# The samples' block compressor as rounded high and low parts, with the pages held stationary

## The chip, the cores and the metric

The kernel runs on one core of a Trainium2 chip. The metric is the device time of one execution in microseconds (us). TensorE (PE in the profile, its weight loads PEld) multiplies, VectorE (DVE), ScalarE (ACT) and GpSimd (POOL) work elementwise, and SyncE (SP) issues all DMAs of this stage.

## What is computed

The reference is one inference step of a two-layer decoder trunk: 1024 prompt tokens, and 8 samples of 8 new tokens each with 1024 cached tokens in 8 pages. In each layer, attention heads work beside an RWKV-7 recurrence. One attention branch reads compressed blocks. The part that the change touches is this:

```python
def compress_blocks(rows, pe, w1, w2):
    b, length = rows.shape[:2]
    n_cmp = (length - CMP_BLOCK) // CMP_STRIDE + 1        # blocks of 32 rows, stride 16: 63
    idx = jnp.arange(n_cmp)[:, None] * CMP_STRIDE + jnp.arange(CMP_BLOCK)[None, :]
    blocks = jnp.take(rows, idx, axis=1) + pe[:, None, :]
    flat = blocks.transpose(0, 1, 3, 2, 4).reshape(b, n_cmp, NSA_KV_HEADS, CMP_BLOCK * HEAD_DIM)
    return jax.nn.silu(flat @ w1) @ w2
...
    k_cmp = compress_blocks(kv_all[:, :, 0], pe[0], w1[0], w2[0])
    v_cmp = compress_blocks(kv_all[:, :, 1], pe[1], w1[1], w2[1])
```

For keys and for values, and for each of two head groups, 63 blocks of 32 x 64 = 2048 numbers go through w1 (2048 x 256), SiLU and w2 (256 x 64). All is float32.

## The kernel before

Each layer runs four stages, one after the other with a barrier between: `projections`, `scan_with_samples`, `prompt_mixing` (the prompt's attention) and `dense_layer`. The change lies in the second, which holds three programs: the scan of the recurrence over the prompt (8 pairs of chunks, 19 steps a pair), the samples' attention (`sample_...`), and a short one for the samples' own chunk of the recurrence (`chunk_...`). Each program is a generator on each engine, and `turns` (L911) fixes their order in advance: 10 rounds of chunk and scan steps, and after them one scan step and one sample step in each round. An engine carries out its list strictly in order, so an instruction that waits holds all that stand behind it.

In a pair's 19 scan steps, steps 1 and 2 are gram steps (L1282 to L1294), step 3 multiplies by G (L1304), steps 4 to 13 are matrix steps of 32 products (L1314 and L1326 in turn, with ScalarE's copy L1387 after the one and VectorE's sum and transpose L1459, L1461 after the other), and steps 14 to 19 are three for each chunk (L1334; L1341; L1348 to L1358).

The samples' program goes over nine requests: eight samples and, as the ninth, the prompt, of which only the compressor runs. A request is 16 steps. Its compressor runs in the first eight:

- SyncE loads a request's pages ahead, into `sa_kvp` (two buffers).
- GpSimd (`sort_rows`, L1817) sorts their keys and values into `sa_kvc`, all four (key or value, group) parts in four copies of 512 elements, while the request before is still in its later steps.
- TensorE turns them (L1529): 8 transposes in each of steps 0 and 1. ScalarE (L1646) and VectorE (L1734) copy each half from PSUM to `sa_kt`.
- TensorE multiplies (L1540): for keys and values, for each half of the 256 hidden columns, 16 fp32 products with a 128 x 128 piece of `cp_w` (w1) stationary and 126 columns of `sa_kt` moving, laid over steps 2 to 7. The hidden values come out with the hidden index on the partitions, which is what w2 needs.
- ScalarE applies SiLU (L1658) into `sa_hid`, with the bias that comes from pe and w1 (`weigh`, L1708), and TensorE multiplies by w2 (L1567, L1571) in step 8.

Meanwhile the prompt's queries and keys (`qT`, `ksT`, `kwT`) and its values (`vs`, `vw`) lie in SBUF untouched, since `prompt_mixing` reads them. At the end of the ninth request SyncE loads the constants and rows which that stage needs first (L1499, L1500). The other matrix stages already work in high and low parts: a float32 number is rounded to fp32r (the high part) and what is left is the low part, and three products replace one: high x high, low x high, high x low. In `projections`, L538 is such a product, with a slice of the input stationary and 256 or 280 columns of weights moving.

Of the kernel before, what the change touches and what calls it, by code (L numbers as in the profile page):

```python
# [21 lines left out]
F32R = mybir.dt.float32r  # L22
# [5 lines left out]
P = 128  # L28
# [879 lines left out]
ROWS_IN = 16 * (PAGES + 3)  # L908

# [14 lines left out]
def scan_with_samples(nc, ps, cst, l, first, first_in, early, early_in, rows_early_in, scan_kept, wend, kcz, vcz, qT, gate, ptab, A, O, X):  # L924
# [8 lines left out]
    sample_names = ("row_in0 row_in1 sorted q_sorted cm_in gates_in prepared weighed bias_done bias_kept k_turned k_even k_odd hidden hid_ready sel_turned "  # L933
# [7 lines left out]
    with Scope(nc) as sc, stage(nc, f"{scan_names} {sample_names} {chunk_names}") as (block, *sems):  # L941
# [7 lines left out]
        (row_in0, row_in1, sorted_, q_sorted, cm_in, gates_in, prepared, weighed, bias_done, bias_kept, k_turned, k_even, k_odd, hidden, hid_ready, sel_turned,  # L949
# [8 lines left out]
        region = sc.sb("sc_region", [P, 13600])  # L958
        kvp2, kvc, kt, ksT, wT = sc.place(base, (("sa_kvp", [P, 2, 4, 1024]), ("sa_kvc", [P, 4, 4, P]), ("sa_kt", [P, 4, 8, 64]), ("sa_ksT", [P, 2, 512]), ("sa_wT", [P, 272])))
# [10 lines left out]
        egmask, seqt, seqp = (eoff[name] for name, _ in parts)  # L970
        w1 = sc.sb("cp_w1", [P, 2, 16, 256])
        w2 = sc.sb("cp_w2", [P, 2, 2, HD])
# [511 lines left out]
        def sample_sync(sp):  # L1484
# [3 lines left out]
            for c in range(NB + 1):  # L1488
# [5 lines left out]
                for n in range(7 if c == NB else 9):  # L1494
                    yield
                if c == NB:
                    sp.wait_ge(hidden, 4 * (NB + 1))
                    a = CO[MIX_CONSTANTS[0]][0]
                    sp.dma_start(early[0][:, :], const_d[:, a:a + MIX_WIDTH]).then_inc(early_in, 16)  # L1499
                    load_ahead(sp, early, rows_early_in, l, A, X)  # L1500
                    yield
                    yield
                    return
# [5 lines left out]

        def sample_tensor(pe):  # L1510
# [3 lines left out]
            for c in range(NB + 1):  # L1514
                u = c % 2
                kvp, wk, kn, wn = kvp2[:, u], wk2[:, u], kn2[:, u], wn2[:, u]
                for i in range(2):
                    if i == 0:
                        pe.wait_ge(sorted_, c + 1)
# [4 lines left out]
                    else:  # L1524
                        pe.wait_ge(w1_in, 96)
                    for kg in (2 * i, 2 * i + 1):
                        for n in range(4):
                            o = (4 + kg) * BANK + n * P
                            m = pe.transpose(ps[:, o:o + P], kvc[:, n, kg, :], cst["ident"])  # L1529
# [1517 lines left out]
```

## Time and profile before

| | |
|---|---|
| median of 3 runs | 3989.98 us (3989.86 to 3991.4) |
| profiled execution | 3985.85 us, its span 3984.1 us |
| granted clock, mean of the span | 0.981 of 2.4 GHz |
| busy: TensorE, VectorE, ScalarE, GpSimd | 3807, 2006, 1124, 1701 us |
| scan stage of the first layer | up to about 846 us |
| first page transposes, first and second layer | 431.96 and 2409.28 us |

A row of the profile's groups names the line of the kernel, the engine, the operation, what is written and what is read, and the count; then busy time and the mean of one; then the time the engine idled just before, and what ended it. A matmul's recorded duration includes the way through the array, so pitches are read from starts. An fp32 product is recorded as two.

### The profile page before, as it was taken

The numbers are of one execution on the slowest core, as the hardware profiler recorded it, in microseconds if no ns is written. First come the engines' busy times: TensorE is split into PE (matmuls) and PEld (weight loads), VectorE is DVE, ScalarE is ACT, GpSimd is POOL, SyncE is SP. The second block draws the span as 40 slices with busy tenths as digits, with TensorE's granted clock in tenths as the row PEclk, the third lists the DMA queues.
The fourth block names the chain that finished last, engine by engine and source line by source line (L and its number), as shares of the span: only waits on it lengthen the run. The fifth ranks groups of instructions, "written<-read, shape, count | busy, mean of one in ns | idle before, by whom it ended". The sixth has DMA issues, their size and how long they took to land. (4 is left out here: it accounts for less than half of the span.)

```text
span 3984.1 us, 83564 instructions
## 1 busy us (share of the span) xinstructions
PE 3807.4 (96%) x34199; PEld 3487.8 (88%) x34199; DVE 2006.2 (50%) x4501; ACT 1124.3 (28%) x2486; POOL 1701.1 (43%) x2284
## 2 busy tenths in 40 slices
PE   8998999989999999999999989999899999999998
PEld 8987788866699999999999877888665999999998
DVE  6587544457545414414556874444574454144153
ACT  3154233347731000100212532333477210000012
POOL 5633222136754434434355421222377644344342
PEclk9998999999999999999999999999999999999998
DMA  4255433220042131131323554332200411311313
GB/s 131 85 163 168 130 88 87 70 97 7 13 124 66 43 127 54 43 138 40 113 93 92 162 172 107 85 88 71 96 9 12 139 54 45 136 43 57 124 39 99
DMA packets 204334, 349.62 MB, mean 88 GB/s; under 512 B 73410, under 2 KB 138050, under 8 KB 203074
## 3 DMA queue, kind: packets, MB, share of 16 engines
q1 hardware_dynamic: 203954, 344.29, 27.7%
q8 instruction: 271, 4.44, 0.5%
q14 instruction: 109, 0.89, 0.1%
HBM read 253.03 MB, written 95.90 MB: 88 GB/s over the span
## 5 line engine op out<-in xcount | busy, mean ns | idle before, releaser
L2644 POOL CAST wr_hi<-wr_raw 128x256 fp32r<-128x256 f32 x584 | 262.8, 450 | 894.3 <-PE ps L2680 888.8
L2646 POOL TENSOR_TENSOR wr_lo<-wr_raw,wr_hi 128x256 fp32r<-128x256 f32 x584 | 548.6, 939 | 46.7
L2680 PE MATMUL ps<-xh,wr_hi 128*128 128x384 f32 x2064 | 453.7, 328 | 0.0
L2680 PE MATMUL ps<-xh,wr_lo 128*128 128x384 f32 x2064 | 453.1, 327 | 0.0
L2680 PE MATMUL ps<-xl,wr_hi 128*128 128x384 f32 x2064 | 452.9, 327 | 0.0
L1409 POOL TENSOR_TENSOR rc_CT<-rc_AT,rc_masks 128x256 f32<-128x256 f32 x192 | 135.6, 724 | 527.6 <-DVE rc_AT L1444 409.3
L2747 ACT ACTIVATE de_c<-de_c 128x1088 f32<-128x1088 f32 (+1 forms) x44 | 49.1, 1116 | 1098.1 <-DVE de_c L2857 1098.1
L2680 PEld LDWEIGHTS ps<-xh,wr_hi 128*128 128x128 f32 x2064 | 348.9, 188 | 0.3
L2680 PEld LDWEIGHTS ps<-xl,wr_hi 128*128 128x128 f32 x2064 | 349.0, 188 | 0.0
L2680 PEld LDWEIGHTS ps<-xh,wr_lo 128*128 128x128 f32 x2064 | 348.7, 188 | 0.0
L2680 PE MATMUL ps<-de_mixh,wr_hi 128*128 128x384 f32 (+1 forms) x1440 | 317.8, 329 | 8.1 <-DVE de_mixl L2782 8.1
L2680 PE MATMUL ps<-de_mixh,wr_lo 128*128 128x384 f32 (+1 forms) x1440 | 317.4, 329 | 0.0
L2680 PE MATMUL ps<-de_mixl,wr_hi 128*128 128x384 f32 (+1 forms) x1392 | 308.5, 329 | 0.0
L2797 DVE TENSOR_TENSOR de_x<-de_x,ps 128x384 f32<-128x384 f32 x168 | 79.3, 527 | 448.0 <-PE ps L2680 448.0
L1540 PE MATMUL ps<-sa_kt,cp_w 128*128 128x126 f32 x2304 | 285.7, 280 | 0.0
L1540 PEld LDWEIGHTS ps<-sa_kt,cp_w 128*128 128x128 f32 x2304 | 265.3, 192 | 7.3
L2243 POOL TENSOR_SCALAR at_s<-at_s,at_fac,gate 128x384 f32<-128x384 f32 (+3 forms) x320 | 209.8, 668 | 126.2 <-DVE at_fac L2225 124.9
L2680 PEld LDWEIGHTS ps<-de_mixh,wr_hi 128*128 128x128 f32 x1440 | 246.8, 189 | 8.6 <-issue 8.6
L2680 PEld LDWEIGHTS ps<-de_mixh,wr_lo 128*128 128x128 f32 x1440 | 247.6, 188 | 0.0
L2680 PEld LDWEIGHTS ps<-de_mixl,wr_hi 128*128 128x128 f32 x1392 | 235.7, 188 | 0.0
L538 PE MATMUL ps<-pr_wh,xh 128*128 128x256 f32 (+1 forms) x720 | 214.7, 298 | 4.2 <-ACT pr_turns L714 2.7
L538 PE MATMUL ps<-pr_wl,xh 128*128 128x256 f32 (+1 forms) x720 | 207.0, 287 | 0.0
(453 smaller groups left out, 7555.2 us busy)
## 6 DMA issues: line engine op xcount, KB each, us to landing
sa_kvp<-in_cache SPq DMA_DIRECT2D x128, 256.0 KB
scr_xres<-de_x SPq DMA_DIRECT2D x56, 544.0 KB, 2.7
de_x<-scr_xres SPq DMA_DIRECT2D x56, 544.0 KB, 3.6
wr_raw<-in_w_gate SPq DMA_DIRECT2D x42, 512.0 KB, 3.6
wr_raw<-in_w_up SPq DMA_DIRECT2D x42, 512.0 KB, 3.7
rc_arbk<-scr_arbk SPq DMA_DIRECT2D x32, 512.0 KB, 4.7
wr_raw<-in_w_down SPq DMA_DIRECT2D x32, 512.0 KB, 3.6
pr_raw<-in_w_rw SPq DMA_DIRECT2D x28, 512.0 KB, 4.4
```

Of the source, the lines that this page charges most:

```text
L538: mm = pe.matmul(ps[0:m, b:b + w], x[:, k, t * P:t * P + m], weights(y, i)[:, k, :], start=(k == 0 and j == 0), stop=(k == KD - 1 and j == 2))
L1409: pool.tensor_tensor(CT[:, n % 2, s], AT[:, s], mid(lev[:, n * CH:(n + 1) * CH], 4), ALU.mult).then_inc(ct_ready[s], 1)
L1540: m = pe.matmul(ps[:, b:b + 126], w1[:, kv, q, half * P:(half + 1) * P], kt[:, 2 * kv:2 * kv + 2, q % 8, q // 8:q // 8 + 63], start=(q == ...
L2243: pool.tensor_scalar(x, x, fac[:, job % 6, g:g + 1], gate[:, o + g:o + g + 1], ALU.mult, ALU.mult).then_inc(normed, 1)
L2644: pool.tensor_copy(hi[:, k, :], raw[:, k, :]).then_inc(w_hi, 1)
L2646: pool.tensor_tensor(lo[:, k, :], raw[:, k, :], f32(hi[:, k, :]), ALU.subtract).then_inc(w_ready, 1)
L2680: m = pe.matmul(ps[:, (bank + b) * BANK:(bank + b) * BANK + cols], w[:, k, :], x[:, k, o:o + cols], start=(k == 0 and i == 0), stop=(k == ...
L2747: act.activation(c[rows, :], c[rows, :], ACT.Silu).then_inc(silu_done, 1)
L2797: m = dve.tensor_tensor(to[:, o:o + w], x[:, o:o + w], ps[:, (bank + b) * BANK:(bank + b) * BANK + w], ALU.add)
```

## The change

The compressor's products become fp32r products in three passes with the operands' parts exchanged: 127 columns of pages (both groups side by side) stationary, 256 columns of w1 moving. The result has the blocks on the partitions, and ScalarE copies it out and TensorE turns it back by two transposes for keys and two for values, ahead of SiLU. ScalarE casts w1 to its high part in eight pieces at the start of the samples' program, and GpSimd subtracts to get the low part, four pieces ahead of the first sort and four beside the first request. VectorE makes the low part of the pages by two more operations per half. The sort works on half a request at a time in a buffer of half the size, so its second half waits for the first half's transposes. The high part of w1 lies where `qT` and the keys and values lay; `qT`, `ksT` and `kwT` are written to memory (`xmT`) at the stage's start and read back at its end, and `vs` and `vw` are read again from outputs that hold them.

```diff
+BLOCK = 20
+BLOCK_PRODUCTS = [(kv, i, q) for kv in range(2) for i in range(3) for q in range(16)]
+WEIGH_ORDER = [(kv, q) for q in range(10) for kv in range(2)] + [(kv, q) for kv in range(2) for q in range(10, 16)]
...
+        w1h = [rounded_at("cp_w1h", [P, 16, 256], at) for at in high_at]
+        w1l = [rounded_at("cp_w1l", [P, 16, 256], w1_at + kv * 16 * 256 * 4) for kv in range(2)]
...
     def sample_sync(sp):
...
-                for n in range(7 if c == NB else 9):
+                for n in range(5 if c == NB else 9):
                     yield
                 if c == NB:
+                    sp.wait_ge(spilled, 48)
+                    sp.wait_ge(raw_done, 2 * NB + 1)
+                    sp.dma_start(qT[:, :, 0:SEQ], xmT[0:4, :, 0:SEQ].rearrange("h p t -> p h t")).then_inc(early_in, 16)
+                    yield
+                    yield
+                    sp.wait_ge(raw_done, 2 * NB + 2)
+                    sp.dma_start(kwT_all[:, 0:SEQ], xmT[5, :, 0:SEQ]).then_inc(early_in, 16)
                     sp.wait_ge(hidden, 4 * (NB + 1))
                     a = CO[MIX_CONSTANTS[0]][0]
                     sp.dma_start(early[0][:, :], const_d[:, a:a + MIX_WIDTH]).then_inc(early_in, 16)
+                    sp.dma_start(ksT_all[:, 0:SEQ], xmT[4, :, 0:SEQ]).then_inc(kept_in, 16)
+                    sp.dma_start(vw[:, 0:SEQ]..., winr[0:SEQ, P:2 * P]...).then_inc(kept_in, 16)
+                    sp.dma_start(vs[:, 0:SEQ]..., kvrows[l, 0:SEQ, 256 + P:512]...).then_inc(kept_in, 16)
                     load_ahead(sp, early, rows_early_in, l, A, X)
...
+        def turn_hidden(pe, c, kv):
+            pe.wait_ge(raw_kept, 2 * c + kv + 1)
+            for half in range(2):
+                o = (5 + 2 * kv) * BANK + half * P
+                pe.transpose(ps[:, o:o + 127], ksT[0:127, 0, 256 * kv + half * P:256 * kv + (half + 1) * P], cst["ident"][0:127, 0:127]).then_inc(hidden, 1)
...
     def sample_tensor(pe):
...
+                    pe.wait_ge(sorted_, 2 * c + i + 1)
...
-                for kv in range(2):
-                    for half in range(2):
-                        b = (4 + 2 * kv + half) * BANK
-                        for part in range(2):
...
-                            for q in range(8 * part, 8 * part + 8):
-                                m = pe.matmul(ps[:, b:b + 126], w1[:, kv, q, half * P:(half + 1) * P],
-                                              kt[:, 2 * kv:2 * kv + 2, q % 8, q // 8:q // 8 + 63], start=(q == 0), stop=(q == 15))
...
+                for n in range(0, 96, BLOCK):
+                    for kv, i, q in BLOCK_PRODUCTS[n:n + BLOCK]:
+                        if i == 0 and q == 0:
+                            pe.wait_ge(k_even, 2 * c + kv + 1)
+                            pe.wait_ge(k_odd, 2 * c + kv + 1)
+                        if c == 0 and i != 1 and q % 4 == 0:
+                            pe.wait_ge(w_low if i else w_high, 4 * kv + q // 4 + 1)
+                        x, w = ((kth, w1h[kv]), (ktl, w1h[kv]), (kth, w1l[kv]))[i]
+                        m = pe.matmul(ps[0:127, (4 + 2 * kv) * BANK:(4 + 2 * kv) * BANK + 256], x[:, kv, q % 8, :, :]...[:, q // 8:q // 8 + 127],
+                                      w[:, q, :], start=(i == 0 and q == 0), stop=(i == 2 and q == 15))
...
+                    if n == 3 * BLOCK:
+                        turn_hidden(pe, c, 0)
+                    yield
+                turn_hidden(pe, c, 1)
+                yield
...
     def sample_scalar(act):
+            act.wait_ge(w1_in, 96)
+            act.wait_ge(spilled, 48)
+            act.wait_ge(q_sorted, 1)
             for n in range(4):
+                for j in (2 * n, 2 * n + 1):
+                    kv, q = j // 4, j % 4 * 4
+                    act.copy(w1h[kv][:, q:q + 4, :], w1[:, kv, q:q + 4, :]).then_inc(w_high, 1)
                 yield
...
+                for kv in range(2):
+                    act.wait_ge(raw_done, 2 * c + kv + 1)
...
+                    act.copy(ksT[0:127, 0, 256 * kv:256 * kv + 256], ps[0:127, (4 + 2 * kv) * BANK:(4 + 2 * kv) * BANK + 256]).then_inc(raw_kept, 1)
...
     def sample_vector(dve):
...
-                    dve.tensor_copy(kt[:, kg], ps[...]).then_inc(k_odd, 1)
+                    dve.tensor_copy(kth[:, i, :, 1], ps[...]).then_inc(odd_high, 1)
+                    dve.wait_ge(odd_high, 2 * c + i + 1)
+                    dve.tensor_tensor(ktl[:, i, :, 1], ps[...], f32(kth[:, i, :, 1]), ALU.subtract)
+                    dve.wait_ge(k_even, 2 * c + i + 1)
+                    dve.tensor_tensor(ktl[:, i, :, 0], ps[...], f32(kth[:, i, :, 0]), ALU.subtract).then_inc(k_odd, 1)
...
     def sample_pool(pool):
+            def low_weights(j):
+                kv, q = j // 4, j % 4 * 4
+                pool.wait_ge(w_high, j + 1)
+                pool.wait_ge(weighed, WEIGH_ORDER.index((kv, q + 3)) + 1)
+                pool.tensor_tensor(w1l[kv][:, q:q + 4, :], w1[:, kv, q:q + 4, :], f32(w1h[kv][:, q:q + 4, :]), ALU.subtract).then_inc(w_low, 1)
...
             for n in range(4):
+                if n < 2:
+                    low_weights(2 * n)
+                    low_weights(2 * n + 1)
                 yield
-            sort_rows(0)
+            sort_rows(0, 0)
             for c in range(NB + 1):
+                sort_rows(c, 1)
                 for n in range(9):
+                    if c == 0 and 1 <= n <= 4:
+                        low_weights(3 + n)
                     yield
...
                     if n == 0:
-                        sort_rows(c + 1)
+                        sort_rows(c + 1, 0)
...
     @block.sync
+            sp.dma_start(xmT[0:4, :, 0:SEQ].rearrange("h p t -> p h t"), qT[:, :, 0:SEQ]).then_inc(spilled, 16)
+            sp.dma_start(xmT[4, :, 0:SEQ], ksT_all[:, 0:SEQ]).then_inc(spilled, 16)
+            sp.dma_start(xmT[5, :, 0:SEQ], kwT_all[:, 0:SEQ]).then_inc(spilled, 16)
...
 in prompt_mixing, attention_tensor, scores(i):
+                if i == 0:
+                    pe.wait_ge(early_in, early_count)
+                if i == R4:
+                    pe.wait_ge(kept_in, 48 * (l + 1))
```

## Rows read from the trace of the kernel before

**Rows 1.** The page, its first part: busy us and share of the span.
```profile
PE 3807.4 (96%) x34199; PEld 3487.8 (88%) x34199; DVE 2006.2 (50%) x4501; ACT 1124.3 (28%) x2486; POOL 1701.1 (43%) x2284
```

**Rows 2.** Busy us by engine in three stretches, granted clock, DMA share.
```profile
core 0: us, PE busy (x) PEld busy (x) DVE busy (x) ACT busy (x) POOL busy (x), PEclk, DMA share, GB/s
410.00:420.00 10.00, 5.86 (x72) 3.45 (x71) 7.99 (x19) 1.95 (x3) 6.62 (x5) 0.77 0.27 73
440.00:840.00 400.00, 385.67 (x6521) 339.93 (x6521) 170.30 (x531) 137.01 (x321) 87.04 (x130) 1.00 0.29 76
2420.00:2820.00 400.00, 385.67 (x6519) 339.75 (x6520) 170.16 (x534) 136.58 (x321) 87.09 (x130) 1.00 0.28 75
```

**Rows 3.** TensorE's waits between 450 and 840 us: total, times, longest.
```profile
PE ps L1314 <- DVE rc_XX L1461: 4.0, 5, 1.5
```

**Rows 4.** Groups of instructions by line: the compressor's products.
```profile
L1540 PE MATMUL ps<-sa_kt,cp_w 128*128 128x126 f32 x2304 | 285.7, 280 | 0.0
```

**Rows 5.** Order of time on TensorE, start and duration, around 616 and 630 us.
```profile
616.21 0.69 PE L1348 MATMUL ps<-rc_UV,rc_bkr 128*64 128x64 f32 x16 [0.69 <-DVE rc_UV L1472]
...
617.95 1.16 PE L1282 MATMUL ps<-rc_arbk 64*128 64x128 f32 x16
...
620.24 0.71 PE L1622 MATMUL ps<-cbuf,sa_s 64*128 64x64 f32 x8
...
630.51 1.15 PE L1326 MATMUL ps<-rc_XX,rc_ys 64*64 64x64 f32 x32
631.59 2.05 PE L1540 MATMUL ps<-sa_kt,cp_w 128*128 128x126 f32 x16
633.57 1.15 PE L1314 MATMUL ps<-rc_XX,rc_CT 64*64 64x64 f32 x32
```

**Rows 6.** Order of time on TensorE in the projections, first and last of ten.
```profile
199.83 0.28 PE L538 MATMUL ps<-pr_wh,xl 128*128 128x256 f32 x1
...
200.91 0.28 PE L538 MATMUL ps<-pr_wh,xl 128*128 128x256 f32 x1
```

**Rows 7.** Groups of instructions by line: the pages' transposes.
```profile
L1529 PE MATMUL ps<-cbuf,sa_kvc 128*128 128x128 f32 x288 | 40.6, 286 | 4.6 <-POOL sa_kvc L1817 4.6
```

**Rows 8.** Groups on GpSimd by line and form.
```profile
L483 POOL TENSOR_TENSOR pr_wl<-pr_raw,pr_wh 128x256 fp32r<-128x256 f32 x112 | 141.0, 1259 | 9.0
...
L483 POOL TENSOR_TENSOR pr_wl<-pr_raw,pr_wh 128x512 fp32r<-128x512 f32 x32 | 43.9, 1372 | 2.6
L1817 POOL COPY sa_kvc<-sa_kvp 128x512 f32<-128x512 f32 x72 | 41.1, 613 | 87.0 <-DMA sa_wn<-scr_winr 87.0
...
L1821 POOL COPY sa_q<-qT 128x256 f32<-128x256 f32 x2 | 0.8, 389 | 0.0
```

**Rows 9.** Groups on ScalarE and on VectorE by line and form.
```profile
L1387 ACT COPY rc_ys<-ps 128x256 f32<-128x256 f32 x60 | 22.2, 372 | 45.7 <-PE ps L1314 43.6
...
L1373 ACT COPY rc_bkr<-ps 128x512 f32<-128x512 f32 x14 | 8.1, 579 | 0.0
...
L1439 DVE TENSOR_TENSOR rc_G<-ps,rc_masks 128x512 f32<-128x512 f32 x28 | 18.0, 686 | 26.3 <-PE ps L1282 26.3
...
L2751 ACT CAST de_mixh<-de_h 128x1088 fp32r<-128x1088 f32 x42 | 46.4, 1104 | 191.6 <-DVE de_h L2865 191.6
```

**Rows 10.** Order of time at the start of the samples' program, both layers.
```profile
423.76 0.84 ACT L1387 COPY rc_ys<-ps 128x256 f32<-128x256 f32 x2 [10.07 <-PE ps L1314]
...
431.96 1.51 PE L1529 MATMUL ps<-cbuf,sa_kvc 128*128 128x128 f32 x8 [1.72 <-POOL sa_kvc L1817]
...
2399.89 0.84 ACT L1387 COPY rc_ys<-ps 128x256 f32<-128x256 f32 x2 [9.74 <-PE ps L1314]
...
2409.28 1.97 PE L1529 MATMUL ps<-cbuf,sa_kvc 128*128 128x128 f32 x8 [2.92 <-POOL sa_kvc L1817]
```

**Rows 11.** Order of time at the stage's end.
```profile
842.93 1.09 SPq L1259 DMA_DIRECT2D scr_yr<-rc_yo  x2
...
846.14 1.65 PE L2115 MATMUL ps<-kwT,qT 64*128 64x384 f32 x4 [3.70 <-PEq L169]
```

**Rows 12.** DMA issues between 820 and 846 us: KB, us to landing.
```profile
ro_rk<-scr_rk SPq DMA_DIRECT2D x1, 2176.0 KB, 9.5
```

More of the change, by code:

```diff
@@ L957, in scan_with_samples, with rounded_at @@
         base = nc.sbuf_base
-        region = sc.sb("sc_region", [P, 13600])
-        kvp2, kvc, kt, ksT, wT = sc.place(base, (("sa_kvp", [P, 2, 4, 1024]), ("sa_kvc", [P, 4, 4, P]), ("sa_kt", [P, 4, 8, 64]), ("sa_ksT", [P, 2, 512]), ("sa_wT", [P, 272])))
+        region = sc.sb("sc_region", [P, 14336])
+        kvp2, _, ksT, kvc = sc.place(base, (("sa_kvp", [P, 2, 4, 1024]), ("sa_kt_at", [P, 2, 4, 8, 64]), ("sa_ksT", [P, 2, 512]), ("sa_kvc", [P, 4, 2, P])))
+        wT, = sc.place(high_at[1] + 16384, (("sa_wT", [P, 272]),))
+        def rounded_at(name, shape, at):
+            return nc.alloc_sbuf_tensor_at(f"{name}_{next(_NUMBER)}", shape, F32R, offset=at)
+        kth, ktl = (rounded_at(name, [P, 2, 8, 2, 64], base + 4 * (8192 + 2048 * i)) for i, name in enumerate(("sa_kth", "sa_ktl")))
         (_, _, eG, eAT, eCT, eXX, eys, ep1, ebkr, eUV, eGV, eyo, eAM, eS8, emasks) = sc.place(base, (
@@ new lines, in sample_tensor @@
+                for n in range(0, 96, BLOCK):
[6 more added lines that the diff above has]
+                        x, w = ((kth, w1h[kv]), (ktl, w1h[kv]), (kth, w1l[kv]))[i]
+                        m = pe.matmul(ps[0:127, (4 + 2 * kv) * BANK:(4 + 2 * kv) * BANK + 256], x[:, kv, q % 8, :, :].rearrange("p g c -> p (g c)")[:, q // 8:q // 8 + 127],
+                                      w[:, q, :], start=(i == 0 and q == 0), stop=(i == 2 and q == 15))
+                        if i == 2 and q == 15:
+                            m.then_inc(raw_done, 1)
+                    if c == 0 and n == 0:
+                        pe.wait_ge(weighed, 32)
+                        for k in range(4):
+                            m = pe.matmul(ps[:, BD + k:BD + k + 1], wsum[:, k * P:(k + 1) * P], cst["ones"][:, 0:1], start=True, stop=True)
+                        m.then_inc(bias_done, 1)
+                    if n == 3 * BLOCK:
+                        turn_hidden(pe, c, 0)
+                    yield
@@ L2937, in trunk @@
                 projections(nc, ps, cst, cbuf, ptab, carried, l, first, first_in, qT, ksT, kwT, vs, vw, gate, wend, kcz, vcz, A, O, X)
-                scan_with_samples(nc, ps, cst, l, first, first_in, early, early_in, rows_early_in, scan_kept, wend, kcz, vcz, qT, gate, ptab, A, O, X)
+                scan_with_samples(nc, ps, cst, l, first, first_in, early, early_in, rows_early_in, kept_in, scan_kept, wend, kcz, vcz, qT, ksT, kwT, vs, vw, high_at, gate, ptab, A, O, X)
                 tail = Scope(nc)
@@ L2941, in trunk @@
                 ring = WeightRing(nc, tail)
[L2942 removed]
+                prompt_mixing(nc, ps, cst, l, early, early_in, rows_early_in, kept_in, scan_kept, home, ring, mixT, kcz, vcz, qT, ksT, kwT, vs, vw, gate, A, X)
             with tail:
```

84 lines of the change are left out of this document (41 added, 43 removed).

## The prediction

> **What bounds the kernel now.** I read the busy time of the page first [rows 1], then the stretches with their granted clock [rows 2], then what TensorE waits for in the stretch of the change [rows 3], then groups and the order of time there. TensorE is busy for 96% of the span. In the scan stage of either layer (about 423 to 846 us, 2399 to 2825 us) it is busy for 386 of 400 us, equal in both layers, while VectorE, ScalarE and GpSimd are at 170, 137 and 87, and the granted clock is 1.00, the 2.4 GHz level [rows 2]. The longest wait of TensorE there is 4.0 us in total, in 390 us [rows 3]. So TensorE's program order sets the time: what is taken from its instructions shortens the stage one for one, and every wait put in its way lengthens it. That cuts both ways here, since the change removes products and adds waits.
>
> **The products.** A request (there are nine per layer, the ninth being the prompt) has 2 x 2 x 16 = 64 fp32 products of 126 columns, each recorded as two passes. 2304 records are 1152 products, busy 285.7 us [rows 4]: 0.248 us each, 15.87 us per request. The order of time agrees: 8 products (16 records) every 1.98 us [rows 5]. After, it has 2 x 3 x 16 = 96 fp32r products, 127 columns stationary, 256 moving. The projections run this very form, a stationary slice of the input under 256 moving columns of rounded weights, at one start per 0.12 us [rows 6]. 96 x 0.12 = 11.52 us. 4.35 us less per request, 18 requests: **-78.4 us**. The granted clock was 1.00 in those rows as in the scan stage, so none of this rests on the clock. The page "TensorE: Matmul & The Clock Gate" of the Trainium skill (section "LDWEIGHTS (loading the stationary operand)") gives a load by its columns, columns over 1.2, in ns: an estimate of 107 ns for 128 columns, which would leave no room below 0.11; by it alone the term would be some 23 us larger than by the row, and the row decides.
>
> **The turn back.** Four fp32 transposes per request of 128 columns; the 288 that turn the pages are busy 40.6 us, 0.141 each [rows 7]. 72 x 0.141: **+10.2**. The pages' own 16 transposes stay.
>
> **Sorting in halves.** GpSimd now sorts half a page set, and the second half's copies wait until TensorE has turned the first half. Before, all was sorted long ahead. A copy of 512 elements takes 0.613, one of 256 0.389 [rows 8]; four of 256 are 1.54, and with 0.1 us allowed for each of two handovers 1.75 us. TensorE has just one scan step to cover it. The two generators run one step each per round, so request c's first step stands behind scan step 15 + 16c of a cycle of 19. The covering steps are, for c = 0 to 8: state and output 1.74, matrix step 1.08 four times, gram 2.29 (start to next start, [rows 5]), twice a step with half a matrix step's products, 0.54, matrix step 1.08. The uncovered rests are 0, 4 x 0.67, 0, 2 x 1.21, 0.67: 5.8 per layer, **+11.6**. Behind the waiting transposes stands all of TensorE's program.
>
> **The turn back's wait.** The transposes of the second half wait until ScalarE has copied the raw sums, and that copy (0.372 for 256 columns, [rows 9]) stands behind ScalarE's own scan step. Where that step is a matrix step it has two copies of 0.372, so TensorE waits about 0.95 (requests 4 and 6); behind the gram step it has two of 0.37 and one of 0.579 [rows 9], 1.9 us (request 7); behind the step that copies rc_GV (512 columns), 1.15 us (request 0); elsewhere nothing, but the step's cover of 2 us has shrunk to 0.3 and VectorE's add and transpose come late by 0.4 and 0.3 (requests 5 and 8). 5.65 per layer, **+11.3**. The first half's transposes stand behind 20 further products and are covered. Silu of the second half then comes late once (0.75 per layer).
>
> **VectorE's two subtractions.** Each half gets a copy and two subtractions of 512 columns out of PSUM, 0.686 each by the nearest rows [rows 9]: 2.06 where 0.69 stood. The products wait for them, but one more half's turn and two scan steps lie between (at least 3 us). What can come late is the next matrix step, which needs VectorE's transposes; followed in order it is 0.3 us for each of two requests, 0.6 per layer. With silu's 0.75: **+2.7**. All VectorE's additions are 18 x 4 x 0.686 = 49 us on an engine that is busy for 170 in 400.
>
> **The start of the stage.** 3 MB are written out of SBUF, ahead of 2 MB of copies; by 410 to 420 us the DMA engines stood at 0.27 [rows 2], so there is room. I cost the write at nothing; were it late it would hold ScalarE's first cast. ScalarE casts w1 in eight pieces of 1024 columns. It can start only behind its own scan copies that end at 424.6 [rows 10]: 1.04 us each by its cast of 1088 columns [rows 9]. GpSimd subtracts: fp32r subtraction of 512 columns takes 1.372 [rows 8], so 2.74 per piece, an estimate. Four pieces stand ahead of the first sort: 424.6 + 1.04 + 10.98 + 1.54 = 438.2, where the first transposes started at 431.96 behind a wait of 1.72 [rows 10]. +6.3. In layer 2 the same sum from 2400.7 gives 2414.4 against 2409.3 [rows 10]: +5.1. TensorE then idles for some 8 us, and the clock had fallen by idling just before (0.77 at 410 to 420, [rows 2]); I put 1 us per layer on it. **+13.4**. Bounds: nothing, if GpSimd is through before TensorE; at 1.259 us per 256 columns [rows 8], 5.0 per piece, +9 more per layer. I take the 512 row, since VectorE is lightly used then. The four later pieces (11 us) run beside two turns, four steps of products and two gram steps, over 19 us: hidden.
>
> **The end.** The queries (2 MB) are read back once the first half's last product is through, some 12 us of TensorE's work plus 3.7 of barrier [rows 11] ahead of attention. 2176 KB landed in 9.5 us [rows 12]: hidden. kwT and the constants are asked for about where the constants were, behind the last turn; ksT, vs and vw (1.5 MB) serve later scores, a dozen us on. SyncE issues four more DMAs at about 0.5 us ahead of the last writes (two took 1.09, [rows 11]), most of it while it would have waited: **+1.0**; bounds 0 and 10 (1.5 MB in front of the loads of the next stage).
>
> Sum: -78.4 + 10.2 + 11.6 + 11.3 + 2.7 + 13.4 + 1.0 = -28.2 us. The profiled execution took 3985.85 (span 3984.1); 3957.7. The median is 4.1 above it: **3962 us**.
>
> **Rivals.**
> *All waits covered* (the added steps run in time already there): -78.4 + 10.2 = -68, 3922 us. For it: all three other engines are under half busy. Against: program order, not load, makes the waits.
> *GpSimd slowed by VectorE: slower than before.* The 256-column subtraction took 1.259 where the 512-column one took 1.372 [rows 8], so GpSimd has no fixed price. Were its copies doubled (0.77) and its pieces 5.0 us, sorts add 13 and the start 9 per layer: +44 on -28, 4002 to 4006 us. It decides once these two exceed 14 us per layer. Against: the sort's copies have a mean of 0.613 over all 72. The page "SBUF — State Buffer" of the Trainium skill (section "Who interferes with whom") says that a VectorE instruction with two SBUF inputs keeps GpSimd from reading; VectorE's new subtractions have one input in PSUM, and by that rule they would not do it; the weighing sums and scan copies would.
> *Products paced by more than 0.12 us.* Mixed among semaphores and scan steps they could start every 0.165, as 384 columns do. Then 96 take 15.84, no gain, and the costs stay: +50, 4040 us. It decides from a pitch of 0.136. Against it the rows of the same form [rows 6].
>
> **Chances.** The forecast 0.62, all covered 0.11, GpSimd slowed 0.18 (half of it ending within 0.2%), products paced 0.09. 0.2%, 8 us, is about what a measurement of this kernel tells from no change. Faster 0.71, same 0.12, slower 0.17. The range takes in most of the covered case and the slowed one up to its middle: 3932 to 4000. The forecast's own range is 3945 to 3980.
>
> **What would show it.** The new products at 0.12 us starts and 11.5 per request; L1529's line waiting for sa_kvc about 0.7 us in eight of nine requests; the turn-back waiting for ScalarE in four; GpSimd's pieces at 2.7; the first page transposes some 6 us later behind the scan step; attention's start as far behind the last scan output as now (3.7 us). The prediction would be wrong if the pieces or sorts cost twice their row, if the spill holds the casts, or if attention waits for the read back.

## The result and the profile after

The changed kernel takes 4020.03 us (median of 6 runs, 4012.53 to 4025.36) beside 3989.92 of the kernel before on the same chip: ratio 1.0076, 95% interval 1.0064 to 1.0088. It is slower by three quarters of a per cent, where 3962 with a range of 3932 to 4000 was forecast. The profiled execution took 4020.03 us too (span 4018.2), 34.1 us more in span than that of before. Executions of one and the same kernel differ by up to 23 us, so the median of a few runs places a kernel only to within several us; where an effect is smaller, the stretches of the traces decide.

The page of the changed kernel, its first part, answers to [rows 1], and the busy time by stretch to [rows 2]:

```profile
PE 3785.8 (94%) x33695; PEld 3459.7 (86%) x33695; DVE 2071.2 (52%) x4573; ACT 1145.3 (29%) x2538; POOL 1747.5 (43%) x2372
```

```profile
core 0: us, PE busy (x) PEld busy (x) DVE busy (x) ACT busy (x) POOL busy (x), PEclk, DMA share, GB/s
410.00:420.00 10.00, 5.14 (x97) 4.32 (x97) 9.75 (x21) 1.95 (x3) 5.89 (x5) 0.87 0.55 167
440.00:840.00 400.00, 370.01 (x6184) 320.87 (x6183) 202.21 (x573) 137.69 (x333) 103.04 (x170) 0.96 0.30 78
2420.00:2820.00 400.00, 363.61 (x6142) 313.11 (x6140) 203.72 (x577) 144.29 (x340) 112.40 (x174) 0.97 0.33 86
```

TensorE is busy for 21.6 us less of the span than before, so work was taken from it. But in the scan stage it now stands still for 30 and 36 us of 400, where it stood for 14, and the granted clock of these stretches is 0.96 and 0.97, no longer 1.00. TensorE's waits in the whole span, total, times and longest, with the groups of the products and the pages' transposes behind them:

```profile
PE ps L1557 <- POOL sa_kvc L1873: 20.8, 15, 6.2
PE ps L2184 <- PEq L169: 17.2, 2, 9.4
...
PE ps L1326 <- DVE rc_XX L1473: 12.9, 20, 1.5
PE ps L1346 <- DVE rc_S L1489: 11.5, 4, 5.5
...
PE ps L1536 <- ACT sa_ksT L1691: 8.1, 8, 1.6
```

```profile
L1568 PE MATMUL ps<-cp_w1h,sa_kth 128*127 128x256 f32 x576 | 84.0, 295 | 0.0
L1568 PE MATMUL ps<-cp_w1l,sa_kth 128*127 128x256 f32 x576 | 81.3, 288 | 0.0
L1568 PE MATMUL ps<-cp_w1h,sa_ktl 128*127 128x256 f32 x576 | 79.0, 284 | 0.0
L1557 PE MATMUL ps<-cbuf,sa_kvc 128*128 128x128 f32 x288 | 41.4, 290 | 20.8 <-POOL sa_kvc L1873 20.8
```

The products are busy for 244.3 us, 0.141 each, where 285.7 stood in [rows 4] and 207 was forecast. A line-by-line comparison of totals doesn't say where the time was lost. A comparison by place does: the first product of the scan stage, the first page transposes of each request and attention's first products are found in the order of time on TensorE in both traces, and the stretches between them are subtracted. The stage of the second layer begins here, before and after:

```profile
2346.63 2.08 PE L1065 MATMUL ps<-sc_arbk 64*128 64x128 f32 x16 [5.89 <-DMA sc_vT<-scr_xmT]
```

```profile
2371.01 2.08 PE L1077 MATMUL ps<-sc_arbk 64*128 64x128 f32 x16 [5.62 <-DMA sc_vT<-scr_xmT]
```

Beside each difference stands what the prediction's own terms give for that stretch.

| stretch | layer 1, before to after | layer 2, before to after | both | forecast |
|---|---|---|---|---|
| start: stage's first product to first page transposes | 60.23 to 66.61 | 62.65 to 65.35 | +9.1 | +13.4 |
| request 0 | 51.15 to 61.05 | 52.48 to 60.53 | +18.0 | -5.3 |
| requests 1 to 6 | 284.01 to 277.21 | 284.00 to 275.75 | -15.1 | -30.4 |
| request 7 | 47.89 to 52.04 | 47.89 to 49.85 | +6.1 | -1.4 |
| request 8 to attention | 31.13 to 36.77 | 30.90 to 35.19 | +9.9 | -4.6 |
| the other stages | | | +6.1 | 0 |
| sum | | | +34.1 | -28.3 |

The start costs less than was forecast. The steady requests gain, by half of what was said. Request 0 and the end are losses where gains were expected. Of the other stages' 6.1 us, 5.0 lie between attention in layer 1 and the stage's start in layer 2: 1500.5 us before, 1505.5 after, and 1500.4 to 1506.7 in the traces of the experiments. The change adds two waits to attention there, for what is read back, but experiments 2 and 8 have them too and take 1500.4 and 1500.5; so this part varies from execution to execution.

### The profile page after: what moved, and what is told of

Its sections match the earlier page's. It is cut to its first block and busy times, and to the rows that moved or that the text cites. A ratio compares the mean times of both kernels' runs of the same rounds, so it can differ in the third digit from the quotient of the medians.

```text
span 4018.2 us, 82840 instructions
## 1 busy us (share of the span) xinstructions
PE 3785.8 (94%) x33695; PEld 3459.7 (86%) x33695; DVE 2071.2 (52%) x4573; ACT 1145.3 (29%) x2538; POOL 1747.5 (43%) x2372
## 5 line engine op out<-in xcount | busy, mean ns | idle before, releaser
L538 PE MATMUL ps<-pr_wh,xl 128*128 128x256 f32 (+1 forms) x720 | 207.2, 288 | 0.0
L483 POOL TENSOR_TENSOR pr_wl<-pr_raw,pr_wh 128x256 fp32r<-128x256 f32 (+2 forms) x152 | 197.7, 1301 | 12.2
```

What stands on the lines that cost most here:

```text
L483: pool.tensor_tensor(lo[:, k, :], src[:, kr, :], f32(hi[:, k, :]), ALU.subtract).then_inc(w_ready, 1)
L538: mm = pe.matmul(ps[0:m, b:b + w], x[:, k, t * P:t * P + m], weights(y, i)[:, k, :], start=(k == 0 and j == 0), stop=(k == KD - 1 and j == 2))
```

## The experiments

**1 and 2. The end, and request 0's pieces.** The first moves the loads of ksT, vw and vs out of the scan stage's last SyncE steps, to the first issues of the attention stage:

```diff
                     sp.dma_start(early[0][:, :], ...).then_inc(early_in, 16)
-                    sp.dma_start(ksT_all[:, 0:SEQ], xmT[4, :, 0:SEQ]).then_inc(kept_in, 16)
-                    sp.dma_start(vw[:, 0:SEQ]..., winr[0:SEQ, P:2 * P]...).then_inc(kept_in, 16)
-                    sp.dma_start(vs[:, 0:SEQ]..., kvrows[l, 0:SEQ, 256 + P:512]...).then_inc(kept_in, 16)
```

> The changed kernel with one edit: the reads of ksT, vw and vs (1.5 MB) are issued by SyncE first thing in the attention stage, not in the scan stage ahead of ro_rk. Theory (SyncE's issues back up behind 1.5 MB more in its queue, and the barrier waits for its last issue): the wait before the first attention score falls from 9.4 us to about 4 in either layer, 10 to 11 us less in all, against the changed kernel's 4020 about 4009. Rival (the barrier waits for the queries' read or for TensorE's own late turn-back): the wait stays at 9 and the time stays at 4020. A loss is possible if the later scores then wait for ksT: up to 5 us per layer at the first score with ksT.

Measured: 4011.35 us (4000.83 to 4012.17), ratio 1.0042 (1.0023 to 1.0061), 8.7 less than the changed kernel where 10 to 11 were expected; the wait before attention's first products falls from 9.4 to 3.4, as expected. The order of issues on SyncE's queue shows the mechanism, first in the changed kernel:

```profile
853.35 4.04 SPq L1521 DMA_DIRECT2D vs<-out_kvrows  x1
857.44 3.56 SPq L2971 DMA_DIRECT2D ro_rk<-scr_rk  x1
...
862.53 1.18 SPq L1271 DMA_DIRECT2D scr_yr<-rc_yo  x2
...
865.55 1.65 PE L2184 MATMUL ps<-kwT,qT 64*128 64x384 f32 x4 [9.42 <-PEq L169]
```

and with the loads later:

```profile
845.71 0.43 SPq L2971 DMA_DIRECT2D ro_rk<-scr_rk  x1
...
849.92 1.09 SPq L1271 DMA_DIRECT2D scr_yr<-rc_yo  x2
...
852.86 0.92 PE L2181 MATMUL ps<-kwT,qT 64*128 64x384 f32 x4 [3.42 <-PEq L169]
```

With the loads ahead, the issue of vs lasts 4.04 us, and the next (ro_rk) 3.56 instead of 0.43, and the scan's last rows (scr_yr), for which the switch of stage waits, leave SyncE 7 us after TensorE's last scan products (855.80). Request 8 to attention is 36.77 and 35.19 with the loads there and 30.80 and 31.10 without, as before (31.13, 30.90). So these three loads in front of the last writes make up all that this stretch lost against before. TensorE did not wait for the read back itself: qT was asked for at 842.38 and lands in 8.1 us (median of the page's part on DMA issues).

The second puts GpSimd's last four low pieces of request 0 two steps later in its program:

```diff
-                    if c == 0 and 1 <= n <= 4:
-                        low_weights(3 + n)
+                    if c == 0 and 3 <= n <= 6:
+                        low_weights(1 + n)
```

> The changed kernel with one edit: GpSimd's last four low pieces of w1 stand two steps later in the first request (steps 3 to 6, not 1 to 4), away from VectorE's last weighing sums and its product with the decay. Theory (a GpSimd piece of 2.4 us holds VectorE's instructions with two inputs in SBUF): the three weighing sums take 1.3 us again where they took 5.1, rc_S's product 0.42 for 2.12, TensorE's wait of 5.0 us before L1346 goes to under 1; 5 us less per layer, 10 in all, if the last products do not wait for their low pieces (at most 2 us). Rival (VectorE is only late because the request started late, and the half clock makes the rest): the sums stay long, nothing gained.

Measured: 4015.36 us (4010.1 to 4018.66), ratio 1.0064 (1.0043 to 1.0084), 4.7 less than the changed kernel where 10 were expected, and the two intervals overlap. Request 0 takes 61.30 and 61.86 us, no less than 61.05 and 60.53. The trace shows that the edit did not move in time what it was meant to move. GpSimd meets nothing to wait for between the sort and the third step, so the first two of the four pieces start right behind the sort as before, and VectorE's sums stand beside them for the same 5.13 us:

```profile
439.99 4.84 POOL L1863 TENSOR_TENSOR cp_w1l<-cp_w,cp_w1h 128x1024 fp32r<-128x1024 f32 x2
```

```profile
440.50 5.13 DVE L1752 SCALAR_TENSOR_TENSOR sa_pT<-cp_w,cp_pe,sa_pT 128x256 f32<-128x256 f32 x3
445.55 0.41 DVE L1487 TENSOR_TENSOR rc_S<-rc_S,ps 128x256 f32<-128x256 f32 x1
446.00 0.42 DVE L1489 TENSOR_TENSOR rc_S<-rc_S,wend 128x256 f32<-128x256 f32 x1
```

The scaling of rc_S now has no piece beside it and takes 0.42 us, where it took 2.12. TensorE's wait for rc_S fell from 11.5 to 7.9 us in all, and in its place the products wait for the two pieces that did come later (at 465.4 and 470.5 us):

```profile
PE ps L1346 <- DVE rc_S L1489: 7.9, 4, 3.6
...
PE ps L1568 <- POOL cp_w1l L1863: 6.2, 2, 3.1
```

So this run speaks for the theory in the one operation that it freed, and leaves the sums untested; experiment 9 tests them.

**3. One sort.** GpSimd's second sort is left out and the values' compressor gets the keys' pages.

```diff
             def sort_rows(c, kv):
+                if kv:
+                    return
...
-                    pe.wait_ge(sorted_, 2 * c + i + 1)
+                    pe.wait_ge(sorted_, c + 1)
```

> The changed kernel with one edit: GpSimd sorts only the first half of each request, and both halves are turned from it, so that the values' compressor gets the keys' pages. Theory (TensorE waits for the second sort for 4.5 us per layer in requests 1 to 8, little more in request 0, and these waits are all that the split costs): 9 to 13 us less than the changed kernel's 4020, so about 4009. Rival (the waits only move to the next instruction, or GpSimd's copies slow others): under 4 us.

Measured: 4004.38 us (3999.76 to 4014.0), ratio 1.0049 (1.0033 to 1.0064), 15.7 less than the changed kernel where 9 to 13 were expected. TensorE's wait for sa_kvc falls from 20.8 to 12.4 us, all of it at the two starts, so the sorts in halves cost 8.4 us of waits. Only a part of these returns: requests 1 to 6 take 274.04 and 274.26, 1.7 and 1.5 less than the 275.75 of the changed kernel's layer 2, while the wait for rc_XX grows from 12.9 to 14.7. The larger part of the gain is in request 0, 55.91 and 55.92. There the missing sort lets GpSimd's pieces start at once, 3.5 us earlier against the page transposes. Only the first of VectorE's three sums still meets one (0.93, 0.49, 0.49 us), and TensorE's wait for rc_S is 3.2 us instead of 5.0. So this gain seems to belong to the pieces and not to the sort.

**4. No low part of the pages.** VectorE's two subtractions are left out, and the second pass takes kth again.

```diff
-                        x, w = ((kth, w1h[kv]), (ktl, w1h[kv]), (kth, w1l[kv]))[i]
+                        x, w = ((kth, w1h[kv]), (kth, w1h[kv]), (kth, w1l[kv]))[i]
```

> The changed kernel with one edit: VectorE's two subtractions per half are left out, and the second pass multiplies the high part of the pages again. The products keep their number and form. Theory (they cost a fraction of a microsecond in two requests): 0 to 5 us less than 4020. Rival (they delay the scan's matrix steps in most requests and take part in the loss of requests 1 to 6): 15 us or more less.

Measured: 4006.29 us (3998.42 to 4013.46), ratio 1.0039 (1.002 to 1.0058), 13.7 less than the changed kernel where 0 to 5 were expected. Requests 1 to 6 take 275.09 and 275.08, 0.7 less than 275.75: the 49 us of subtractions are covered in the steady requests, as forecast. Request 0 gives back 3.0 and 2.3. TensorE's waits for sa_kvc (21.2) and for sa_ksT (8.1) are as before (20.8, 8.1). Requests 0 to 6 together give back 8.1 us in this trace, of which 1.5 (request 1 of layer 1: 48.63 there, 47.1 in most traces) vary between executions; the rest of the 13.7 lies in request 7 and in stages that the edit does not touch. So in request 0, beside the pieces, leaving the subtractions out saves 5.3 us, which the forecast's 2.7 for all requests did not hold; what the rest of the gain is stays open.

**5. All products in one block.** The 96 products stand in the first of the five steps, the other four are left without.

```diff
-                    for kv, i, q in BLOCK_PRODUCTS[n:n + BLOCK]:
+                    for kv, i, q in BLOCK_PRODUCTS if n == 0 else ():
```

> All 96 products of a request stand in one piece instead of five. If the products cost 0.12 us from start to start and the 0.141 us of the changed kernel's busy time per product is what five pieces between scan steps add (a load that cannot run ahead, a scan step's start), their busy time falls to about 0.12 to 0.125 each, 208 to 216 us in all. If 0.128 from start to start is the pace of this form here, whatever stands around it, it stays at 0.128 or above, 221 us or more. The kernel as a whole is slower than the changed one in either case, since the scan steps then stand without products between them.

The kernel takes 4052.17 us in its one run, slower as expected. The products' busy time falls from 244.3 to 228.3 us, 0.132 each. By the marks set beforehand that misses the 208 to 216 and speaks for the slow pace (221 or more). But busy time turns out to be the wrong measure, since it holds the products' tails and those at the lower clock level; the starts say the opposite. The order of time on TensorE for request 4, first there and then in the changed kernel:

```profile
649.44 2.17 PE L1568 MATMUL ps<-cp_w1h,sa_kth 128*127 128x256 f32 x16
...
659.06 2.07 PE L1568 MATMUL ps<-cp_w1l,sa_kth 128*127 128x256 f32 x16
661.06 1.15 PE L1326 MATMUL ps<-rc_XX,rc_CT 64*64 64x64 f32 x32
```

```profile
645.23 2.15 PE L1568 MATMUL ps<-cp_w1h,sa_kth 128*127 128x256 f32 x16
647.22 0.63 PE L1568 MATMUL ps<-cp_w1h,sa_ktl 128*127 128x256 f32 x4
647.78 1.15 PE L1326 MATMUL ps<-rc_XX,rc_CT 64*64 64x64 f32 x32
...
660.04 2.19 PE L1568 MATMUL ps<-cp_w1l,sa_kth 128*127 128x256 f32 x16
662.16 1.15 PE L1326 MATMUL ps<-rc_XX,rc_CT 64*64 64x64 f32 x32
```

In one block 96 products take 661.06 - 649.44 = 11.62 us, 0.121 each: the pitch of [rows 6] holds, and with it the forecast's 11.52. In five blocks they take 2.55 + 2.56 + 2.58 + 2.49 + 2.12 = 12.30 us from the first start of each block to the next line's start, so each further block costs 0.17 us. The other requests agree: 11.61 to 11.63 us in one block and 12.28 to 12.34 in five, in all requests but request 0. Read in the same way, the trace of before gives the old products six stretches, of which the first is [rows 5] (631.59 to 633.57): 1.98 four times and 3.77 twice, 15.46. What a request saves is 15.46 - 12.30 = 3.16 us, not 4.35. The rest of the busy time per product, 0.141 against 12.30 / 96 = 0.128, are the tails of blocks, which lie beside the next line's work, and products at the lower clock level.

**6 and 7. Request 0 in another order, and with it the loads later.** GpSimd makes one low piece, then sorts, then makes the other seven. In request 0 alone the low weights' products stand behind all others, and VectorE's last six weighing sums stand ahead of the pages.

```diff
-                    for kv, i, q in BLOCK_PRODUCTS[n:n + BLOCK]:
+                    for kv, i, q in (BLOCK_PRODUCTS if c else FIRST_PRODUCTS)[n:n + BLOCK]:
...
-                    if n == 3 * BLOCK:
+                    if n == (3 if c else 4) * BLOCK:
                         turn_hidden(pe, c, 0)
...
+            weigh(dve, 26, 32)
...
-                if n < 2:
-                    low_weights(2 * n)
-                    low_weights(2 * n + 1)
+                if n == 0:
+                    low_weights(0)
...
-                    if c == 0 and 1 <= n <= 4:
-                        low_weights(3 + n)
+                    if c == 0 and n < 4:
+                        low_weights(2 * n + 1)
+                        if n < 3:
+                            low_weights(2 * n + 2)
```

> Only request 0 of each layer is arranged otherwise: GpSimd makes one low piece, then sorts, then makes the other seven; the products of the low weights (third pass) stand behind the first two passes of keys and values; VectorE's last six weighing sums stand ahead of the page set. If the losses at the start and in request 0 (12.8 and 18 us in the two layers) come from GpSimd's order and its pieces beside VectorE's work, the first page transposes come about 5 us earlier in layer 1 and in layer 2, and request 0 takes 2 to 5 us less: 14 to 20 us less in the median than the changed kernel, 4000 to 4006. The rival, that the 3 MB written out at that time or the clock after the stage's switch set it: at most 3 us less, request 0 still 8 us longer than before.

Measured: 3993.76 us (3985.74 to 4001.65, 12 runs), ratio 1.0009 (0.9998 to 1.0019), 26 us less than the changed kernel, where 14 to 20 were expected. Request 0 takes 52.35 and 50.88 us. TensorE's waits there, first in the changed kernel (435 to 500 us) and then here (433 to 486):

```profile
PE ps L1557 <- POOL sa_kvc L1873: 6.2, 1, 6.2
PE ps L1346 <- DVE rc_S L1489: 5.0, 1, 5.0
```

```profile
PE ps L1558 <- POOL sa_kvc L1874: 3.9, 1, 3.9
...
PE ps L1347 <- DVE rc_S L1490: 0.8, 1, 0.8
```

The second kernel has the loads of experiment 1 moved as well.

> The arrangement of request 0 as above, together with the three later loads moved behind the switch to the attention stage. If the start, request 0 and the end are separate losses, the gains add: 14 to 20 plus the 8.7 measured for the later loads, 3991 to 3997, level with the kernel before. If they cover each other (an earlier start only means a longer wait later), the time stays above 4002.

Measured: 3981.67 us (3975.36 to 3998.72, 12 runs), ratio 0.998 (0.9968 to 0.9991). The gains add (12.1 us for the loads here, 8.7 alone), the sum is below the 3991 to 3997 expected, and this version is faster than the kernel before, by 0.2%. Its profiled execution is the slowest of its twelve, so its trace is not compared by place.

**8. The memory traffic alone.** The kernel before, with the change's writes at the stage's start and its five loads at the end, at the change's places, and with attention waiting for them; no product is touched.

```diff
+            sp.dma_start(xmT[0:4, :, 0:SEQ]..., qT[:, :, 0:SEQ]).then_inc(spilled, 16)
...
+                    sp.wait_ge(hidden, 4 * NB + 2)
+                    sp.dma_start(qT[:, :, 0:SEQ], xmT[0:4, :, 0:SEQ]...).then_inc(early_in, 16)
```

> The kernel before with the memory traffic of the change alone: queries and keys written out at the start of the scan stage, and all five read back at its end at the places of the change, with attention waiting for them. By the theory that the read back costs only by standing ahead of the stage's last writes on SyncE, 8 to 12 us slower than before for both layers, all between the last request and attention's start, and nothing at the start. The rival, that the traffic also disturbs the scan stage (GpSimd, page rows): more than 14 us, part of it in request 0. The prediction had it at 1 us.

Measured: 4005.99 us (4002.52 to 4017.29), ratio 1.0042 (1.0026 to 1.0059), 16.9 us slower than before. By its size this is the rival's, by its places both have a part. In the trace 10.9 us (6.1 and 4.8) are at the end (37.25 and 35.73 from request 8 to attention), as the theory has it. The rest is in layer 1 alone: the first page transposes 4.4 us later, request 0 1.3 and requests 1 to 6 1.2 longer; in layer 2 the scan stage takes what it took before. TensorE's waits between 380 and 436 us show gaps for which nothing in the profile is named:

```profile
PE ps L1132 <- POOL sc_AM L1180: 2.0, 1, 2.0
PE ps L1123 <- issue: 1.3, 1, 1.3
```

The trace of before has 0.3 there. Behind that gap the granted clock is 0.50, the 1.2 GHz level, from 410 to 420 us, where [rows 2] has 0.77. Each trace has such gaps, of 0.3 to 1.4 us in layer 1, and in layer 2 up to 4.4: there the traces of experiments 1, 7 and 9 each have one of 3.1 to 4.4 us, and their first page transposes come 71.2 to 76.4 us after the stage's first product, where the other traces have 62.6 to 67.7. The traces name a likely source. The profile has a DMA queue of the kind "instruction" (q8), with transfers of 16 KB. All 36 gaps of this sort, of 0.2 us or more, in the scan stages of the eleven traces end soon after such a transfer has landed, 35 of them 1.3 to 1.7 us after and one 2.1. So TensorE seems to have waited for its own instructions, which travelled among much other traffic (the DMA engines' share is 0.6 to 0.9 in the ten microseconds around the long gaps). No experiment takes this apart, and whether the change's writes lengthen the gaps stays open: the trace of before has one of 1.6.

**9. Small pieces.** Each low piece of 1024 columns is made as four instructions of 256.

```diff
-                pool.tensor_tensor(w1l[kv][:, q:q + 4, :], w1[:, kv, q:q + 4, :], ...)
+                for k in range(q, q + 4):
+                    m = pool.tensor_tensor(w1l[kv][:, k:k + 1, :], w1[:, kv, k:k + 1, :], ...)
```

> The changed kernel with each of GpSimd's eight low pieces of 1024 columns made as four instructions of 256. If a VectorE operation with both inputs in SBUF stands until GpSimd's instruction in progress has ended, it now stands for at most one of 256 columns, under 1 us (940 ns at L2715): the three weighing sums take at most 3 x 1.4 = 4.2 us in place of 5.1, and the scaling of rc_S at most 1.4 in place of 2.12; GpSimd's columns cost more each, so its pieces take 3 to 4 us in place of 2.42, the start comes 2 to 6 us later and the median is no better, 4018 to 4032. If instead the two engines share a port column by column, the sums keep their 1.7 us mean and the scaling its 2.1.

The order of time in request 0 of the changed kernel, VectorE's and then GpSimd's, with [idle before]:

```profile
441.82 0.68 DVE L1782 TENSOR_TENSOR sa_ktl<-ps,sa_kth 128x512 fp32r<-128x512 f32 x1
442.42 5.13 DVE L1752 SCALAR_TENSOR_TENSOR sa_pT<-cp_w,cp_pe,sa_pT 128x256 f32<-128x256 f32 x3
447.46 0.42 DVE L1487 TENSOR_TENSOR rc_S<-rc_S,ps 128x256 f32<-128x256 f32 x1
447.92 2.12 DVE L1489 TENSOR_TENSOR rc_S<-rc_S,wend 128x256 f32<-128x256 f32 x1
```

```profile
441.90 4.84 POOL L1863 TENSOR_TENSOR cp_w1l<-cp_w,cp_w1h 128x1024 fp32r<-128x1024 f32 x2
447.17 2.58 POOL L1863 TENSOR_TENSOR cp_w1l<-cp_w,cp_w1h 128x1024 fp32r<-128x1024 f32 x1 [0.43 <-DVE sa_pT L1752]
```

and with small pieces:

```profile
441.98 2.23 DVE L1752 SCALAR_TENSOR_TENSOR sa_pT<-cp_w,cp_pe,sa_pT 128x256 f32<-128x256 f32 x3
444.14 0.41 DVE L1487 TENSOR_TENSOR rc_S<-rc_S,ps 128x256 f32<-128x256 f32 x1
444.58 0.50 DVE L1489 TENSOR_TENSOR rc_S<-rc_S,wend 128x256 f32<-128x256 f32 x1
```

```profile
441.47 12.34 POOL L1864 TENSOR_TENSOR cp_w1l<-cp_w,cp_w1h 128x256 fp32r<-128x256 f32 x16
```

Taken one by one, the three sums of the changed kernel last (shortest, median, longest, in ns):

```profile
L1752 DVE SCALAR_TENSOR_TENSOR sa_pT<-cp_w,cp_pe,sa_pT x3: 485/2127/2447, 442.4 to 447.1; 128x256 f32<-128x256 f32 x3
```

The two long ones end 0.28 us after the piece that had started before them (444.54 after 444.26, 447.03 after 446.74), and the scaling of rc_S too (450.03 after 449.75). The short one has no piece beside it.

GpSimd works through both stretches, and its columns cost more here (0.77 us per 256, 3.1 per 1024, where the whole piece took 2.42). Yet VectorE's sums fall from 1.71 to 0.74 us each and the scaling of rc_S from 2.12 to 0.50. So VectorE does not share with GpSimd column by column: an operation of VectorE with both inputs in SBUF stands until GpSimd's instruction in progress is over. GpSimd pays a little as well: a piece of 256 columns takes 0.73 us alone and 0.90 where one of these operations came beside it, and the whole pieces take 2.36 alone and 2.52 to 2.58 there. Request 0 falls to 54.71 and 56.14 us, 10.7 less in both layers together. The median is 4012.56 us (4003.79 to 4021.74), ratio 1.0056 (1.0039 to 1.0073), 7.5 less than the changed kernel and below the 4018 to 4032 expected: the start was costed (the first wait for the sort grew from 6.2 to 7.7), what request 0 gives back was not.

## Why the prediction was wrong

**The product term was mis-sized.** It was -78.4 us: 15.87 per request before, 11.52 after. Both ends were off in the same direction. The 15.87 was a sum of busy time, which holds each block's tail beside the next line; from start to start it is 15.46. The 11.52 was the pitch of a long run, right to 1% for one block (11.62), but the products stand in five blocks at 0.17 more for each (12.30). The term measures 18 x 3.16 = -56.9, so 21.5 us of the forecast gain never were there. This is all that is wrong with requests 1 to 6: 12 x 1.19 = 14.3 of the 15.3 us between forecast and trace. The rival "products paced by more than 0.12 us" had the right place; at 0.128 it stays below the 0.136 from which it decides. (Its 0.165 is the pace of the dense stage's products, a third of which have 320 columns and not 384.)

**"The four later pieces: hidden" is the step that failed most.** They are hidden from GpSimd's side, at 2.42 us where 2.74 was put. But VectorE, behind them, is not. Its three weighing sums take 5.13 us instead of 1.26 and the scaling of rc_S 2.12 instead of 0.42; TensorE stands 5.0 us for rc_S with its program behind it, and then has the lower clock, as the order of time and the busy time by stretch show (columns as above):

```profile
450.08 1.12 PE L1346 MATMUL ps<-rc_S,rc_arbk 64*64 64x64 f32 x16 [4.99 <-DVE rc_S L1489]
451.14 3.78 PE L1568 MATMUL ps<-cp_w1h,sa_kth 128*127 128x256 f32 x16
```

```profile
445.00:450.00 5.00, 0.09 (x1) 0.00 (x0) 4.93 (x5) 0.59 (x1) 4.32 (x2) 0.81 0.85 205
450.00:455.00 5.00, 4.92 (x34) 4.80 (x35) 3.94 (x9) 0.00 (x0) 1.14 (x1) 0.51 0.16 36
455.00:460.00 5.00, 5.00 (x66) 4.71 (x65) 0.59 (x2) 0.37 (x1) 1.23 (x1) 1.00 0.00 0
```

Idle for five microseconds, TensorE comes back at a granted clock of 0.51 (1.2 GHz), and the first 16 products take 3.78 us instead of 2.15. In layer 1 the lower clock costs request 0 about as much as the waits do. The waits are 5.9 us longer than before (rc_S 5.0, sa_ksT 1.0). Counted against the same lines before, about 1.3 us of lower clock lie ahead of the wait for rc_S, about 2.0 right behind it, and 2.9 from 491 us on, where the granted clock is 0.50 from 492.5 to 499.3 us. In both layers that last stretch comes some 53 us into the request; before, there is none in layer 1 and one half as long in layer 2. No experiment takes this last one apart. Request 0 came out 23.3 us above its forecast, both layers taken together; the term above explains 2.4 of it. Experiment 9, which changes nothing but the length of GpSimd's instructions, gives 10.7 back: this much is shown to be VectorE's standing for GpSimd, with the clock that follows from it. Experiment 6, which keeps all pieces and all products and changes only the order, gives 18.4 back. The rival "GpSimd slowed by VectorE" was the right pair of engines with the roles turned round: GpSimd's copies (0.400 us for 256 columns, where 0.389 was put) and pieces (2.42, where 2.74 was put) kept near their price or below it, and VectorE paid. The page "SBUF — State Buffer" of the Trainium skill (section "Who interferes with whom") says that the shared port pair is an exclusive lock, that a VectorE instruction with two SBUF inputs contends for it with a GpSimd instruction that reads SBUF, and that issue order decides who is blocked; the prediction used this for one direction alone. The trace agrees on both: VectorE's operations that read PSUM (L1487, 0.42; L1782, 0.68) run beside the pieces at their usual price, those with two SBUF inputs wait for the piece that began before them. The other direction shows in experiment 6, where two sort copies took 0.60 us instead of 0.40 beside sums of VectorE.

**The end.** +1.0 was put, with 10 as the upper bound for "1.5 MB in front of the loads of the next stage". Request 8 to attention came out 14.5 us above forecast; the product term explains 2.4, and the loads 5.97 + 4.09 = 10.1 (experiment 1). The bound had the right size but the wrong victim: not the next stage's loads but the last scan rows were behind them, and the stage's switch waits for those. Experiment 8 finds the same 10.9 with the products of before.

**The start, near its forecast in layer 1 by luck.** +9.1 for +13.4: 6.4 for 7.3 in layer 1, 2.7 for 6.1 in layer 2. From the end of ScalarE's scan copies to the first page transposes the prediction put 13.6 us; it took 11.9 in both layers, since a piece cost 2.34 to 2.48 us there and not 2.74. Against before that is +4.5 and +3.3, for +6.3 and +5.1. The 2 us put on the clock do not stand there; what the lower clock cost lies in request 0. Instead those copies themselves came 1.9 us later in layer 1, behind two gaps like those of experiment 8 (1.2 and 0.6 us, where before has one of 0.3), and 0.6 earlier in layer 2. The write of queries and keys "at nothing" is neither confirmed nor refuted: experiment 8 has 6.9 us more in layer 1 and nothing in layer 2.

**What was right.** The sort's waits: 8.4 in 13 places for 11.6. The turn back's waits: 8.1 us, 8 times, for 11.3. The turn back's own transposes: 0.68 us per request from start to start, 12.2 in all, for 10.2. VectorE's subtractions: covered in the steady requests. **Request 7** is 7.5 us above its forecast, 2.4 of it the products; there the longest wait for sa_ksT (1.6 us) stands, and the granted clock is 0.90 to 0.93 between 795 and 825 us where it was 1.00. In layer 2 it is 2.0 over before, in the other traces with the new products 1 to 6, so this part varies from execution to execution; no experiment takes it apart.

Sum of the differences: start -4.3, products 21.5, request 0 20.9, end 12.1, request 7 5.1, requests 1 to 6 the remaining 1.0, other stages 6.1: 62.4 us, from -28.3 to +34.1.

## What to carry to other kernels

Cost a saving from start to start at the block length the program will have, not from busy time or a long run: here that alone was 27% of the gain. When work is "hidden" on one engine, ask who shares a port with it: here a VectorE operation with two SBUF inputs waited for the whole GpSimd instruction in progress (up to 2.45 us for 0.49), so long GpSimd instructions belong where VectorE owes TensorE nothing, or must be cut short. An instruction moved to a later step of its engine's program moves in time only if something ahead of it waits (experiment 2), so look at the trace before reading the result. And a load that nobody needs soon still delays what is issued behind it on the same queue, so the last writes of a stage go first.

## What the hardware showed that was not expected

VectorE's standing for GpSimd is as long as GpSimd's instruction: sums of 0.49 us took up to 2.45 beside pieces of 2.42, and 0.74 on average beside pieces of 0.77. A DMA's issue on SyncE's queue, otherwise 0.3 to 0.8 us at the stage's end, lasted 4.04 and 3.56 when loads were queued up (4.78 for the same load in experiment 1, where only later loads stood behind it). One idle stretch of TensorE of 5 us cost about 1.6 us more in the next 16 products through the granted clock. And 36 of 36 pauses of TensorE in the scan stages for which the profile names nothing ended 1.3 to 2.1 us after a 16 KB transfer on the "instruction" queue had landed.
